# Two compression insertions instead of four, score products of both heads in one go, and a second slab of x that skips PSUM

## What is computed

```
hin = _rms_norm(x, norm_g[0]);  z = hin @ w_in
y_moba = _moba_attention(...)      # 4 heads of 64, blocks of 256 keys: here plain causal attention
y_ml   = _mlstm_chunkwise(...)     # 4 heads, after a causal convolution and silu on lq, lk
y_nsa  = _nsa_attention(...)       # 4 heads: compressed, selected and window branch
x = x + _rms_norm(concat(head_norm(...)) @ w_out, norm_g[1])
x = x + _rms_norm(square(relu(_rms_norm(x, norm_g[2]) @ w1)) @ w2, norm_g[3])
```

## Time and profile before

| | |
|---|---|
| median of 3 runs | 606.14 us (605.5 to 606.33) |
| the profiled execution | 605.88 us, of which the span from its first to its last instruction 604.1 us |
| PE busy | 594.5 us, 98% of the span |
| DVE, ACT, POOL busy | 388.0, 300.4 and 256.4 us |
| attention (units 0 to 23) | about 159 to 212 us |

### The profile page before, as it was taken

How to read it: one execution, slowest core, us unless ns; L and a number is a source line. 1 busy time by engine, 2 the same in 40 slices (tenths; PEclk the granted TensorE clock), 3 DMA queues, 4 the chain that set the end, 5 groups by cost and what they waited for, 6 DMA issues and landing times.

```text
span 604.1 us, 8291 instructions
## 1 busy us (share of the span) xinstructions
PE 594.5 (98%) x3099; PEld 485.4 (80%) x3099; DVE 388.0 (64%) x665; ACT 300.4 (50%) x529; POOL 256.4 (42%) x137
## 2 busy tenths in 40 slices
PE   8999999999999999999999999999999999999995
PEld 5898888767867678899878888888888888888884
DVE  6414605265878783883999768586595685771657
ACT  7613423653589933554645536444345255454322
POOL 8553323563095610053357453632723626711611
PEclk9999999999999999999999999999999999999998
DMA  8743281375013820027034250521603404104002
GB/s 331 281 148 131 79 201 73 85 181 187 1 34 79 288 73 0 1 72 278 1 140 139 107 172 1 194 86 43 208 30 139 140 1 147 62 1 174 1 35 106
DMA packets 36580, 67.18 MB, mean 111 GB/s; under 512 B 2876, under 2 KB 23612, under 8 KB 35516
## 3 DMA queue, kind: packets, MB, share of 16 engines
q1 hardware_dynamic: 36236, 66.25, 33.7%
q10 hardware_dynamic: 304, 0.39, 0.3%
HBM read 62.18 MB, written 2.10 MB: 106 GB/s over the span
## 4 chain that ended last, share of the span: by engine, by line
PE 95%; ACT 2%; issue 2%; DVE 1%; POOL 0%; POOLq 0%; ACTq 0%; DVEq 0%
PE ps L1809 20%; PE ps L1811 20%; PE ps L1810 20%; PE ps L2275 7%; PE ps L2277 7%; PE ps L2276 7%; PE ps L2127 2%; PE ps L2142 2%; PE ps L2036 1%; PE ps L2037 1%; ACT probs L946 1%; PE ps L2005 1%; PE ps L1975 1%; PE ps L2203 1%; PE ps L2157 1%
## 5 line engine op out<-in xcount | busy, mean ns | idle before, releaser
L1809 PE MATMUL ps<-xT_h,ring_h 128*128 128x512 f32 (+1 forms) x384 | 144.8, 377 | 0.0
L1811 PE MATMUL ps<-xT_h,ring_l 128*128 128x512 f32 (+1 forms) x384 | 143.3, 373 | 0.0
L1810 PE MATMUL ps<-xT_l,ring_h 128*128 128x512 f32 (+1 forms) x384 | 143.1, 373 | 0.0
L770 POOL TENSOR_TENSOR ring_l<-raw_d,ring_h 128x1024 fp32r<-128x1024 f32 x25 | 67.3, 2700 | 129.9 <-ACT ring_h L1041 129.9
L770 POOL TENSOR_TENSOR ring_l<-raw,ring_h 128x1024 fp32r<-128x1024 f32 x31 | 76.7, 2498 | 77.4 <-DVE xres L1625 38.1
L694 POOL TENSOR_TENSOR ring_l<-raw,ring_h 128x512 fp32r<-128x512 f32 (+2 forms) x26 | 64.2, 2488 | 75.0 <-ACT ring_h L793 75.0
L1719 DVE TENSOR_TENSOR y<-ps,y 128x512 f32<-128x512 f32 x90 | 61.2, 689 | 51.0 <-PE ps L2277 50.6
L1809 PEld LDWEIGHTS ps<-xT_h,ring_h 128*128 128x128 f32 x384 | 72.4, 189 | 15.0 <-issue 2.4
L1811 PEld LDWEIGHTS ps<-xT_h,ring_l 128*128 128x128 f32 x384 | 72.4, 188 | 12.9
L1810 PEld LDWEIGHTS ps<-xT_l,ring_h 128*128 128x128 f32 x384 | 72.4, 189 | 12.3
L2275 PE MATMUL ps<-ring_h,a_h 128*128 128x512 f32 x196 | 76.7, 391 | 0.1
(11 more groups left out here) (277 smaller groups left out, 998.0 us busy)
## 6 DMA issues: line engine op xcount, KB each, us to landing
raw<-in_w_mlp SPq DMA_DIRECT2D x16, 1024.0 KB, 5.5
raw_d<-in_w_mlp SPq DMA_DIRECT2D x16, 1024.0 KB, 6.0
raw<-in_w_groups SPq DMA_DIRECT2D x8, 1024.0 KB, 4.8
xres<-in_x SPq DMA_DIRECT2D x8, 512.0 KB, 6.5
raw<-in_nsa_cmp_w SPq DMA_DIRECT2D x8, 512.0 KB, 6.4
raw<-in_w_groups SPq DMA_DIRECT2D x8, 256.0 KB, 5.0
raw<-in_w_out SPq DMA_DIRECT2D x2, 1024.0 KB, 5.1
raw<-in_w_out SPq DMA_DIRECT2D x4, 512.0 KB, 4.7
```

Source lines behind the costliest of these rows:

```text
L770: nc.gpsimd.tensor_tensor(slot(ring_l, n), slot_source(n), slot(ring_h, n).bitcast(F32), ALU.subtract).then_inc(lo_done, 1)
L1809: nc.tensor.matmul(o, sh, mh, start=start, stop=False)
L1810: nc.tensor.matmul(o, sh, ml, start=False, stop=False)
L1811: return nc.tensor.matmul(o, sl, mh, start=False, stop=stop)
```

## The change

Three edits, none of which changes what is computed.

1. **Second slab of x.** ACT rounds slab 1 straight from `x_land` with the gain as its scale, and DVE gets the low half from `x_land` in one instruction; the pass through PSUM is gone for this slab. DVE's order becomes `x_low(0)`, low half of x slab 1, low half of weight slab 1 (which was POOL's), `x_gain(2)`, and from there as before. ACT does `x_high(1)` ahead of `lv_high(1)`.
2. **Compression.** `compress(0)` and `compress(1)` at k = 3, `compress(2)` and `compress(3)` at k = 7.
3. **Scores.** `scores(u)` issues the products of both heads, and then both masks. It is called once in unit u, for unit u + 2, ahead of `back`, `values` and both `transposes`.

```diff
@@ gpsimd
-            for k in range(NC):
+            for k in (0, *range(2, NC)):
+                if k == 3:
+                    pool.wait_ge(xl_ready, 3)
@@ scalar
             def x_high(k):
-                act.wait_ge(x_scaled, k + 1)
-                nc.scalar.activation(xT_h[:, k, :], ps[:, 4 + k % 4, :], ACT.Copy).then_inc(xh_ready, 1)
+                if k == 1:
+                    act.wait_ge(x_land_in[1], 16)
+                    nc.scalar.activation(xT_h[:, 1, :], x_slab(1), ACT.Copy, scale=gain_cols[:, 1:2]).then_inc(xh_ready, 1)
+                else:
+                    act.wait_ge(x_scaled, max(k, 1))
+                    nc.scalar.activation(xT_h[:, k, :], ps[:, 4 + k % 4, :], ACT.Copy).then_inc(xh_ready, 1)
...
-            for k in range(NC):
+            lv_high(0)
+            x_high(0)
+            x_high(1)
+            lv_high(1)
+            for k in range(2, NC):
@@ vector
             x_gain(0)
-            for k in range(NC):
+            x_low(0)
+            dve.wait_ge(xh_ready, 2)
+            nc.vector.scalar_tensor_tensor(xT_l[:, 1, :], x_slab(1), gain_cols[:, 1:2], xT_h[:, 1, :].bitcast(F32),
+                                           ALU.mult, ALU.subtract).then_inc(xl_ready, 1)
+            dve.wait_ge(hi_first, 2)
+            nc.vector.tensor_tensor(lv_slab(ring_l, 1), lv_slab(raw, 1), lv_slab(ring_h, 1).bitcast(F32), ALU.subtract
+                                    ).then_inc(xl_ready, 1)
+            x_gain(2)
+            for k in range(2, NC):
@@ tensor
-            def quarters(k):
-
-                if k % 2:
-                    compress(k // 2)
+            def halves(k):
+
+                if k in (3, 7):
+                    compress(0 if k == 3 else 2)
+                    compress(1 if k == 3 else 3)
...
-            def score(s):
+            def scores(u):
+
+                products(2 * u)
+                products(2 * u + 1)
+                mask(2 * u)
+                mask(2 * u + 1)
+
+            def mask(s):
+                w = (s // 2 % NT + 1) * P
+                nc.tensor.matmul(ps[:, S_BANK[s % 5], w - P:w], identb[:], mask_s[:], start=False,
+                                 stop=True, skip_group_check=True).then_inc(s_done, 1)
+
+            def products(s):
...
-                nc.tensor.matmul(ps[:, bank, w - P:w], identb[:], mask_s[:], start=False,
-                                 stop=True, skip_group_check=True).then_inc(s_done, 1)
...
             pe.wait_ge(ml_used, 4)
-            score(2)
+            pe.wait_ge(cs_sub, 1)
+            scores(1)
             transposes(0)
-            pe.wait_ge(cs_sub, 1)
-            score(3)
             pe.wait_ge(*reads(J_MK[1]))
             for u in range(NU):
                 g, i = divmod(u, NT)
                 for m in range(2):
                     s = 2 * u + m
-                    if s + 4 < 2 * NU:
-                        score(s + 4)
+                    if m == 0 and u + 2 < NU:
+                        scores(u + 2)
                     if m == 0 and g and i == 3:
                         back(g - 1)
```

More of the change, by code:

```diff
@@ L1843, in first_group @@
                 for k in range(NC):
-                    pe.wait_ge(xl_ready, k + 1)
+                    pe.wait_ge(xl_ready, k + 2 if k else 1)
                     if k % 4 == 3:
                         pe.wait_ge(lo_done, k // 4 + 1)
-                    else:
-                        pe.wait_ge(lv_low, lv_count(k))
+                    elif k != 1:
+                        pe.wait_ge(lv_low, lv_count(k) - (k > 1))
                     for t in range(0 if k else EARLY_LV, NT):
@@ L1885, in _ @@
             first_group()
-            pe.wait_ge(xl_ready, 2 * NT)
+            pe.wait_ge(xl_ready, 2 * NT + 1)
             token_group(J_B, C_B, BN)
@@ L2076, in values_and_scores @@
                 if k == 4:
-                    score(0)
-                    score(1)
+                    scores(0)
                 if k == 5:
@@ L2088, in _ @@
             near_scores(1)
-            half_feature(J_MK[0], C_MK, 0, quarters)
+            half_feature(J_MK[0], C_MK, 0, halves)
             states(0)
```

## The result

| | before | after |
|---|---|---|
| median | 606.04 us (4 runs, 605.5 to 606.33) | 612.55 us (4 runs, 612.43 to 612.83) |
| profiled execution, span | 605.88, 604.1 us | 612.49, 610.8 us |

The ratio is 1.0109 (95% interval 1.0092 to 1.0127): slower by 6.5 us. The forecast was 612.3.

What follows compares the result with a forecast made beforehand. PE, busy for 594.5 of 604.1 us, was taken to bound the kernel. From 605.88 us, -0.25 (start), -0.65 (compression) and +7.1 (scores) gave 612.1, with 0.26 for the median 612.3; range 609.9 to 614.3.

Steps and rivals of the forecast that it cites:

- Part 3: Attention: products wait for exp(2u) ahead of `values`, so PE's and ACT's work follow each other; +7.1 us.
- The ring: Attention, four-unit group: transposes, ACT's exps, products, masks and `values` in series; period 10.5 to 10.6 us instead of 8.59.
- Unit 5: Attention: head 1's products and mask come ahead of the first `values`; +0.6 us.
- The upper bound of +8.3: Attention: loss if the rings gain waits of their own, such as `back` behind exp(2u) at i = 3.
- The sum: Whole kernel: 605.88 - 0.25 - 0.65 + 7.1 = 612.1 us, or 612.3 as a median.
- Part 2: Compression: two calls back to back save two of four prices for going in and out; 0.65 us gained.
- Rival (c): Compression: the switches are not saved, no gain, 613.0 us; a variant within the closed ring's 0.85.
- Part 1: Start: PE's wait for DVE's low half at slab 1 goes; 0.25 us gained, bounds 0 and 0.35.
- the cover of 0.6 us: Start: DVE's low half of the weight slab ends at 7.8, PE needs it at 8.44.
- (a): Attention: the exp is there in time, so only the first two parts count; 605.2 us, chance 0.06.
- (b): Attention: rings close only partly, ACT gets back half, part 3 costs 3.5; 608.7 us, chance 0.07.
- (d): Attention: the order itself is worth -0.5 us apart from waits; 611.8 us, a variant within the closed ring's 0.85.

Runs made afterwards that it cites:

- e1: Kernel before with only the new score order (joint scores ahead of `back` and `values`): 613.78 us, ratio 1.0126.
- e2: Kernel after with the score order of before, so only the start and compression edits: 605.02 us, ratio 0.9981.
- e8: Kernel after with ACT rounding only an eighth of one `w_out` chunk: 610.90 us, ratio 1.0079.
- e11: Kernel after with joint scores only in the five units with i = 1, all others as before: 612.96 us, ratio 1.0111.
- e10: Kernel before with only the compression edit (`halves` for `quarters`): 605.36 us, ratio 0.9988.
- e4: Kernel after with the score order of before in the five units with i = 1, joint scores in all others: 606.87 us, ratio 1.0014.
- e9: Kernel before with only the edits to the start: 606.10 us, ratio 0.9995.
- e3: Kernel after with joint scores issued behind `transposes(2u)` instead of ahead of `back` and `values`: 616.78 us, ratio 1.0177.
- e5: Kernel after with `back` and `values` ahead of the joint scores instead of behind: 611.70 us, ratio 1.0089.
- e7: Kernel after with joint scores behind `transposes(2u)`, as in e3, and DVE doing `copy_t(u)` ahead of `row_max(2u + 4)`: 610.08 us, ratio 1.0059.
- e12: Kernel before with ACT rounding only an eighth of one `w_out` chunk: 607.00 us, ratio 1.0011.

## Why the prediction was right, step by step

**Part 3, its place and kind: right.** e1 has all of the loss, e2 none. The waits stand where they were forecast: at L2067, released by ACT's exp, 1.40, 1.40 and 1.39 us in units 13, 17 and 21 and 0.3 to 0.8 at i = 3. ACT stands for 2.50, 1.98 and 1.98 us under the `values` of these three units, and for 1.59 and 1.30 at the first two; "over 2 us during each" was too much. e8 shows that ACT's time is in series with `values` now, and e11 that the units with `values` are enough. That a matmul doesn't pass a waiting one, on which all hung, the rows show: PE stands for 1.40 us ahead of 189.11 while `values` starts at 189.90, although the last input that it waits for (DVE's addition to `y`) was there at 187.73. By the rule that the prediction took from the Trainium skill (TensorE: Matmul & The Clock Gate, in Step-by-step: what each phase is for), the trace agrees.

**Part 3, its size: 7.75 instead of 7.1.** The ring from 192.21 to 202.88, term by term against the forecast: transposes to exp(29) 0.53 (0.54); ACT to the end of exp(34), 192.74 to 199.73, 6.99 (6.95); release and products 0.63, from 199.73 to 200.36 (about 0.5); masks and switch 0.22 (0.22); `values` 2.30 (2.31). Sum 10.67 against 10.52; the period before was 8.59. The mis-sized term is the release with the products, 0.63 instead of 0.5: 0.06 for the release (199.73 to 199.79), 0.33 for the first product (to 200.12), which is slower behind the wait, and 0.24 for the second. Over four groups the loss came to 42.46 - 35.29 = 7.2 instead of 6.7. Unit 5 cost 0.8 instead of 0.6 (from scores(1) to the first `values`: 158.71 to 169.27 before, 157.57 to 168.91 after), and the end gave back 0.1 instead of 0.2. The upper bound of +8.3 rested on no row.

**The sum: close in part by luck.** The traces differ by 1.08 us of gain ahead of the attention (0.9 forecast) and 7.75 of loss in it (7.1 forecast). These two misses, +0.65 and -0.18, partly cancel, and the median of the kernel after lies 0.06 us over its profiled execution instead of the 0.26 that I added. So the total is off by 0.25 us only.

**Part 2: right.** The timeline after, around the first two calls:

```profile
130.70 0.39 PE L1829 MATMUL ps<-xT_h,ring_l 128*128 128x512 f32 x1
131.02 1.96 PE L1993 MATMUL ps<-raw,blk 64*32 64x256 f32 x64
132.91 0.50 PE L1827 MATMUL ps<-xT_h,ring_h 128*128 128x512 f32 x1
133.25 0.40 PE L1828 MATMUL ps<-xT_l,ring_h 128*128 128x512 f32 x1
```

64 records run as one block, and 130.70 to 133.25 is 2.55 us. Two calls apart would be 2 x 1.68 less the two ordinary steps that only one insertion now holds, 0.46: 2.90. So 0.35 us an insertion, 0.7 in all against 0.65. The stretch from the first matmul of `half_feature` to the first mark says the same: 10.65 us before (129.12 to 139.77), 9.94 after (128.75 to 138.69), and 9.94 in e10 too (129.25 to 139.19). e10's time is 0.8 us shorter, with an interval that takes in 0.7. Rival (c) is out.

**Part 1: as forecast in one execution, and not shown as a gain.** In the profiled execution of the kernel after, slab 1 follows slab 0 without a wait:

```profile
8.05 0.40 PE L1829 MATMUL ps<-ring_h,xT_l 128*128 128x512 f32 x1
8.28 0.39 PE L1827 MATMUL ps<-ring_h,xT_h 128*128 128x512 f32 x1
8.51 0.40 PE L1828 MATMUL ps<-ring_l,xT_h 128*128 128x512 f32 x1
```

It begins 0.31 us earlier than in the earlier trace rows. Of that, 0.15 is slab 0 being earlier altogether (its last matmul at 8.05 instead of 8.20), and 0.16 is the gap that closed (0.23 instead of 0.39); with the faster second matmul (0.23 instead of 0.30) the wait itself was 0.23, against 0.21 in the forecast. But whether slab 1 waits depends on the execution, in both versions. With the new start it waits 0.31 us for DVE's low half of the weights in e2's trace and 1.05 in e4's; with the old start it doesn't wait in e1's, where slab 0 had come late (8.71 to 8.94). And e9 can't be told from no change. The step that was too simple is the cover of 0.6 us: it took x slab 1 as landed. ACT's high half of it, which waits for the transfer, starts at 5.52 us in the kernel after and at 6.96 in e4.

**The rivals.** (a), exp there in time, is refuted by the waits of 1.40 us, and (b), the ring half open, by the periods of 10.7 us, which are those of a closed ring. (d), the order worth something by itself, can't be read from any of these runs: each placing of the joint scores tried (e3, e4, e5, e7) cost 1.8 to 11.8 us over e2, by waits.

**What my experiments got wrong.** I had held that taking the wait out of `values`' way would give the 7.7 us back, whatever else moved. e3, e5 and e7 say no. The order of before has three things around `values`: one score ahead of it, on which DVE works during its 2.3 us; no wait for an exp ahead of it; and right behind it the transposes that ACT wants. The order after loses the second, e3 and e7 the first, e5 the first and the third. Of e7's 5.0 us the two waits for DVE shown above make up 5.1, against 0.3 for the same two in e2's trace. e4's 1.8 us lie in part in the three waits named there; neither was tested further.

## What to carry to other kernels

Ahead of the longest stretch of an in-order engine, count what each other engine has to do while it runs; a wait that was free behind that stretch can cost nearly its whole length when it is moved ahead, once for every turn of the loop (here 2.0 to 2.2 us of 2.3 in units 13, 17 and 21). When instructions are moved on one engine, read the lists of all engines that wait for them: here a copy on DVE stood behind a row maximum that had nothing to do with it, and cost 6.8 us. Insertions in another tile mode cost by the change, so put them together; a gain of 0.3 us in front of arriving data can't be told from the spread of its landing times.

## What the runs showed of the hardware

**A tiny DVE instruction can take as long as POOL's.** The product of 8 columns in `coefficients` (both inputs in SBUF) took 0.17 to 1.28 us. In e12, DVE's and then POOL's timeline:

```profile
191.73 1.28 DVE L1521 TENSOR_TENSOR stat<-stat,gt 128x8 f32<-128x8 f32 x1
193.04 0.89 DVE L1464 TENSOR_REDUCE stat<-ps 128x1 f32<-128x512 f32 x2
...
187.91 5.06 POOL L694 TENSOR_TENSOR ring_l<-raw,ring_h 128x512 fp32r<-128x512 f32 x4 [2.67 <-ACT ring_h L795]
```

POOL's block ends at 192.97, its last instruction of four having started near 191.70, and DVE's product ends at 193.01. In the kernel before, the same two:

```profile
190.90 0.22 DVE L1519 TENSOR_TENSOR stat<-stat,gt 128x8 f32<-128x8 f32 x1
...
188.57 4.98 POOL L694 TENSOR_TENSOR ring_l<-raw,ring_h 128x512 fp32r<-128x512 f32 x4 [4.17 <-ACT ring_h L793]
```

The product ends at 191.12, and POOL's second instruction of four about 191.06 (188.57 + 2 x 4.98 / 4). So a DVE product that comes while POOL works on SBUF ends with POOL's instruction: how long it takes depends on when it comes. Other traces bear it out: in e8 it takes 0.86 us and ends at 192.45, POOL's block at 192.41; in e3 it takes 0.17 us at 186.89, where POOL does nothing. This is the rule of the Trainium skill (SBUF — State Buffer, in SBUF: two separate sides): DVE with two SBUF inputs and GpSimd share a pair of ports that one of them holds for a whole instruction. The traces agree, with 1.28 us beside POOL (e12) against 0.17 without it (e3).

By its rows this accounts for e12: ACT's shorter work lets POOL begin 0.47 us ahead of `values` (187.91 against 188.38) instead of 1.03 behind it (188.57 against 187.54), DVE's product falls at the start of a POOL instruction instead of its end, the row maxima behind it are 1.1 us late (4.66 behind the start of `values` instead of 3.61), and PE waits 0.62 us for an exp:

```profile
194.54 0.63 PE L2129 MATMUL ps<-ident,probs 128*128 128x128 f32 x4 [0.62 <-ACT probs L948]
```

No run took POOL's work away at that place, so the link is read and not tested. In e4 the same product takes 1.28 us at 200.17, ahead of a wait of 0.56 for an exp; that may be some of its 1.8. In e5 it takes 1.25 us at 192.48 and 1.17 at 202.77, instead of 0.22 and 0.18 in e2, just ahead of row maxima for which ACT waits (0.73 and 1.25 us). So up to about 2 of the 6.5 us that e5 costs over e2 may come from when DVE meets POOL, and not from the order around `values`; no run separates the two.

**The start varies more than it can gain.** The row of the two plain float32 matmuls ahead of slab 0 is 2.02 us long in e4 and 3.67 in e9, at a granted clock that reads 1.00 in both, and slab 1 began between 8.03 us (e8) and 9.35 (e12). What makes these two matmuls longer stays open.
